# Weight pieces of the z/gates stage rounded and split in twos, one term's split moved, and the first eight o inputs rounded earlier

## The reference

```python
u = rms_norm(h, norm_g)
proj = u @ w_in                     # 1024 x 7168: q, f, i, g_hg, u_s, z_s, gate_hg, gate_s5
o = rms_norm(hgrn2_mix(q, f, i, lb), hg_norm_g)          # chunked recurrence, 8 heads
y_hg = (o * silu(g_hg)) @ w_o_hg
ys = gelu(s5_mix(u_s, ...))                              # 32 groups, 64 complex states each
ys = glu_a * sigmoid(glu_b) * silu(z_s)                  # glu_a, glu_b from ys @ w_glu + b_glu
y_s5 = ys @ w_o_s5
h = h + (sigmoid(gate_hg) * y_hg + sigmoid(gate_s5) * y_s5) @ w_out
h = h + (p @ w_ple) * sigmoid(rms_norm(h) @ w_ple_gate)
return rms_norm(h)
```

## Time and profile before

| what | value |
|---|---|
| median of 3 runs | 2148.1 us (2147.4 to 2154.41) |
| the profiled execution's own time | 2150.59 us |
| its span | 2149.0 us, mean granted TensorE clock 0.995 |
| PE busy | 2119.0 us (99%) |
| DVE busy | 1555.1 us (72%) |
| ACT busy | 1043.9 us (49%) |
| POOL busy | 292.8 us (14%) |

### The profile page before, as it was taken

The page is one execution under the profiler, slowest core; times in us unless marked ns, Lnnn a source line. Parts: engine busy times, 40 slices in busy tenths (PEclk is TensorE's granted clock), DMA queues, the critical chain, the costliest instruction groups (busy, mean ns, idle before and its releaser), DMA issues.

```text
span 2149.0 us, 29076 instructions
## 1 busy us (share of the span) xinstructions
PE 2119.0 (99%) x10178; PEld 1740.7 (81%) x10178; DVE 1555.1 (72%) x3140; ACT 1043.9 (49%) x1585; POOL 292.8 (14%) x518
## 2 busy tenths in 40 slices
PE   9999999999999999999998999999999999999997
PEld 6788888888888888888876788878888888888886
DVE  7775757777778778788888788566657567666756
ACT  6511245455455555575455455643544454354344
POOL 0011145000000000102322232211002001100100
PEclk9999999999999999999999999999999999999999
DMA  6453389311011011445568455675338435634632
GB/s 213 101 187 121 125 263 207 147 54 54 29 54 54 29 54 44 106 141 187 163 196 304 147 171 157 189 235 180 113 119 260 152 117 192 221 108 130 222 118 79
DMA packets 179598, 308.41 MB, mean 144 GB/s; under 512 B 40400, under 2 KB 85216, under 8 KB 179488
## 3 DMA queue, kind: packets, MB, share of 16 engines
q1 hardware_dynamic: 136816, 195.91, 28.6%
q0 software_dynamic: 38448, 102.69, 15.2%
q10 hardware_dynamic: 4224, 8.39, 1.1%
HBM read 232.33 MB, written 94.37 MB: 152 GB/s over the span
## 4 chain that ended last, share of the span: by engine, by line
PE 94%; DMA 2%; DVE 1%; ACT 1%; issue 1%; SPq 0%; DVEq 0%; ACTq 0%
PE c_bank L390 23%; PE c_bank L391 23%; PE c_bank L392 23%; PE c_bank L1499 6%; PE c_bank L1501 6%; PE c_bank L1500 6%; DMA u_hi<-terms_scratch 2%; PE c_bank L797 1%; PE c_bank L774 1%; PE c_bank L784 1%; PE c_bank L795 1%; PE c_bank L1536 1%; PE c_bank L1539 1%; PE c_bank L1519 1%; DMA x_xs<-x_in 0%
## 5 line engine op out<-in xcount | busy, mean ns | idle before, releaser
L390 PE MATMUL c_bank<-u_hi,c_w_both 128*128 128x512 f32 x576 | 231.9, 403 | 3.9 <-DVE u_hi L1181 1.7
L392 PE MATMUL c_bank<-u_hi,c_w_both 128*128 128x512 f32 x576 | 224.2, 389 | 0.0
L391 PE MATMUL c_bank<-u_lo,c_w_both 128*128 128x512 f32 x560 | 218.5, 390 | 0.0
L2308 ACT ACTIVATE c_w_both<-c_raw 128x1024 fp32r<-128x1024 f32 x91 | 96.6, 1061 | 166.5 <-PE c_bank L392 158.8
L1057 DVE STREAM_TRANSPOSE hg_ken<-hg_ke 32x128 f32<-32x128 f32 x512 | 154.6, 302 | 6.5
L390 PEld LDWEIGHTS c_bank<-u_hi,c_w_both 128*128 128x128 f32 x576 | 108.2, 188 | 34.4 <-issue 5.6
L391 PE MATMUL c_bank<-t_oa_lo,c_w_both 128*128 128x512 f32 (+1 forms) x344 | 132.1, 384 | 0.0
L392 PE MATMUL c_bank<-t_oa_hi,c_w_both 128*128 128x512 f32 (+1 forms) x344 | 132.1, 384 | 0.0
L390 PE MATMUL c_bank<-t_oa_hi,c_w_both 128*128 128x512 f32 (+1 forms) x344 | 132.1, 384 | 0.0
L392 PEld LDWEIGHTS c_bank<-u_hi,c_w_both 128*128 128x128 f32 x576 | 108.2, 188 | 23.0
L864 ACT ACTIVATE hg_S<-hg_G,hg_coef 128x128 f32<-128x128 f32 x120 | 47.5, 401 | 156.8 <-DVE hg_G L1082 110.9
(11 more groups left out here) (392 smaller groups left out, 5656.6 us busy)
## 6 DMA issues: line engine op xcount, KB each, us to landing
c_raw<-sums_scratch SPq DMA_DIRECT2D x80, 256.0 KB, 2.8
c_raw<-w_in_in SPq DMA_DIRECT2D x64, 256.0 KB, 3.8
gates_scratch<-s_stage POOLq DMA_DIRECT2D x64, 256.0 KB, 4.3
t_ein<-gates_scratch SPq DMA_DIRECT2D x64, 256.0 KB, 4.5
c_raw<-w_o_hg_in SPq DMA_DIRECT2D x32, 512.0 KB, 3.6
c_raw<-w_out_in SPq DMA_DIRECT2D x32, 512.0 KB, 3.3
c_raw<-w_ple_gate_in SPq DMA_DIRECT2D x32, 512.0 KB, 3.3
sums_scratch<-w_in_in POOLq DMA_DIRECT2D x60, 256.0 KB, 12.5
```

The costliest lines, as they stand in the source:

```text
L390: pe.matmul(out, w_hi, u_hi, start=first, stop=False)
L391: pe.matmul(out, w_hi, u_lo, start=False, stop=False)
L392: return pe.matmul(out, w_lo, u_hi, start=False, stop=last)
L2308: act.activation(w_hi[u % WS], raw[u % RS], ACT.Copy).then_inc(w_hi_done, 1)
```

## The change

It has three parts.

1. `round_piece` and `split_piece` do nothing for an even q. For an odd q they wait for both loads and handle the pieces q - 1 and q by one instruction over both slots (128x1024), which counts both semaphores up by 2. As `piece(u, i)` stands for 7u + i + 4, the instructions stand at i = 1, 3, 5 in even units and at i = 0, 2, 4, 6 in odd ones.
2. In unit 10 DVE's split of term 7 moves from behind `piece(u, 4)` to ahead of `piece(u, 2)` and `turn_forward`.
3. In the tail before its loop, o inputs 0 to 3 are rounded and split behind units 2 and 3 of `glu`, and 4 to 7 behind units 0 and 1 of `os5`; before, they stood behind units 0 to 3 of `os5`.

```diff
     def round_piece(self, act, q):
-        u, i = divmod(q, PRODS)
-        act.wait_ge(*self.piece_in[q % 4].at(16 * (q // 4 + 1)))
+
+        if q % 2 == 0:
+            return
+        for n in (q - 1, q):
+            act.wait_ge(*self.piece_in[n % 4].at(16 * (n // 4 + 1)))
         if q < 4:
             act.wait_ge(self.head_proj, 3 * (NT * HEADS - 1) + 1 + q // 2)
         else:
             act.wait_ge(*self.prod_done.at(q - 3))
-        act.activation(self.ring(q)[0], self.piece(q), ACT.Copy).then_inc(self.piece_hi.sem, 1)
+        hi, _, raw = self.both_pieces(q)
+        act.activation(hi, raw, ACT.Copy).then_inc(self.piece_hi.sem, 2)
 
     def split_piece(self, dve, q):
-        hi, lo = self.ring(q)
+        if q % 2 == 0:
+            return
+        hi, lo, raw = self.both_pieces(q)
         dve.wait_ge(*self.piece_hi.at(q + 1))
-        dve.tensor_tensor(lo, self.piece(q), hi.bitcast(F32), ALU.subtract).then_inc(self.piece_lo.sem, 1)
+        dve.tensor_tensor(lo, raw, hi.bitcast(F32), ALU.subtract).then_inc(self.piece_lo.sem, 2)
...
+                if u == 10:
+                    quads.split_term(dve, 7)
                 if u not in (0, 10):
                     piece(u, 2)
                 if use:
...
                 piece(u, 4)
-                if u == 10:
-                    quads.split_term(dve, 7)
                 gated(u, C11)
...
             if not body:
-                return [("o", 2 * i), ("o", 2 * i + 1)] if sec == "os5" else []
+                n = i - 2 if sec == "glu" else i + 2
+                return [("o", 2 * n), ("o", 2 * n + 1)] if 0 <= n < 4 else []
```

More of the change, by code:

```diff
@@ L250, with both_pieces @@
     SUM_DMAS, COPY_DMAS = NQ // 2 * 16, 2 * len(COPIED) * 16
+    def both_pieces(self, q):
+        r = q % 4 // 2
+        return self.w.hi[:, r], self.w.lo[:, r], self.w.raw[:, r]
     def round_piece(self, act, q):
-        u, i = divmod(q, PRODS)
-        act.wait_ge(*self.piece_in[q % 4].at(16 * (q // 4 + 1)))
+        if q % 2 == 0:
+            return
+        for n in (q - 1, q):
+            act.wait_ge(*self.piece_in[n % 4].at(16 * (n // 4 + 1)))
         if q < 4:
```

## The result

| | median | runs |
|---|---|---|
| before, measured with it on one chip | 2150.6 us | 2147.4 to 2154.41 (4) |
| changed kernel | 2172.36 us | 2170.96 to 2173.12 (4) |

A forecast was written before the change was run, and what follows sets the result against it. PE was taken as the bound, busy 2119.0 of 2149.0 us. The terms 3.8 + 4.2 + 1.7 + 0.5 + 0.2 - 1.8 gave +8.6 us, so 2156.7 against the median of 2148.1; range 2150.5 to 2163.

The forecast's parts named there:

- Even units, product 4: Six even z/gates units: the pair behind add_c11 starts product 4 late, 0.63 us each, 3.8 us in all.
- Odd units, product 5: Eight odd units, 3 to 17: the pair behind scans makes product 5 late, 0.52 us each, 4.2 us in all.
- Unit 0: Product 6's piece, formerly split ahead of term 3, now stands behind add_c11: 1.7 us later.
- Unit 2: Product 6's piece, formerly first of three, ends later as a pair: 0.5 us, lower bound 0.
- Unit 10: Product 6 waits for a pair behind turn_forward and the moved term 7 split: +0.2 us, bounds -0.8 and +1.5.
- The tail's o inputs: Tail: earlier splits remove PE's wait for o input 6, -1.8 us; bounds -1.8 and 0.
- ACT: ACT's round of a pair in z/gates units: begins early enough to leave over 3 us of cover, so no cost.
- Rival 4: Pairs of loads come late and ACT waits; eight units lose 1 us more each: 2165 us; chance 0.08.
- Rival 3: Clock falls at 14 new stalls, each costing one product at 1.2 GHz: +38 us, 2195 us; chance 0.02.
- Rival 2: Unit 10: earlier piece for product 6 halves the 7.28 us stall and keeps the clock up; 2140.0 us; chance 0.03.
- Rival 5: DVE's total decides: 70 x 0.07 = 5 us go, no stall comes; with the tail -6.7, 2141.4 us; chance 0.01.
- Rival 1: Even and odd units' small stalls too small to be seen, half of 8.0 goes: +4.6, 2152.7 us; chance 0.18.

The follow-up runs named there:

- e4: Changed kernel, loads in its order, but pairs stand earlier on DVE, in unit 10 ahead of the term's split; 2163.54 us, ratio 1.0069.
- e8: Kernel before, rounds and splits single, but SP's load of an even piece waits until both pieces in its two slots are split; 2161.2 us, ratio 1.0057.
- e9: Changed kernel with only unit 7's 2 MB copy load ahead of the load of piece 7u+7; 2166.54 us, ratio 1.0077.
- e1: Changed kernel, but in odd units SP issues U, trig and the copy ahead of the load of piece 7u+7; 2162.47 us, ratio 1.0064.
- e6: Kernel before with the change's third part alone, o inputs rounded and split earlier; 2148.2 us, ratio 0.9992.
- e2: Changed kernel, but in odd units SP loads piece 7u+8 ahead of U, trig and the copy, which stay late; 2163.9 us, ratio 1.0072.
- e5: Changed kernel with the load order of e1 and the pair places of e4 together; 2148.69 us, ratio 0.9994.
- e10: e5 with pieces 0 to 19 single again, pairs from piece 20 on; 2146.82 us, ratio 0.9986.
- e3: Kernel before with the change's second and third parts (term 7's split and o inputs earlier), no pairs; 2145.07 us, ratio 0.9983.

## Why the prediction was right or wrong

- **Even units, product 4**: right. 0.66 to 0.70 for a forecast of 0.63; the pair took the 1.22 us taken from the tail's rows.
- **Odd units, product 5**: place right, size too small. Product 5 began 0.47 to 0.54 late where the sum had 0.44, and 0.14 to 0.19 more was lost in the course of it, where the sum had 0.08: the first matmuls behind a stall follow each other in 0.34, then 0.24 and 0.23 us. In unit 3 product 4 was 0.16 late too. In units 15 and 17 the pair behind `matrices` stood 0.36 us later in the unit than in unit 13, which used up the 0.18 that I had to spare at product 3, and products 3 and 4 together were 0.35 late. 6.4 in place of 4.2. e4 shows the place to be the cause.
- **Unit 0**: right, 1.55 for 1.7. **Unit 2**: 1.4 for 0.5; DVE came to this unit's pair 0.9 later than I had it. It stood behind a result of ACT's (`par_lr`, L1611) until 4.96 us into the unit, 4.15 before.
- **Unit 10**: +0.2 forecast, -2.0 found. The stall at the unit's start gave the loads time, and product 5's wait of 2.74 was gone. Product 6 waited 8.8 us behind the pair, where I had 7.6. e8 and e9, which keep that stall, have the same 33.9 us for the unit. Where it was removed (e1), unit 10 cost 1.2 over before, inside my bounds, but no more than the unit varies by itself.
- **The tail's o inputs**: right, -1.8 on the wait list; its size in the time is not settled by e6.
- **The step that failed** is the one under **ACT**, "Over 3 us of cover remain". It reckoned when the round of a pair may begin by the product four before, and took the load as there, so it put at nothing what came to 13.45 of the 22 us: ACT stood 7.46 and 6.97 us before two rounds, and PE 5.11 and 4.61. I had counted instructions on DVE, ACT and PE, but not what the merged count does to SP: a split that frees two slots at once frees the first later, and in odd units a whole `matrices` later. SP waits for that in order, and U, trig, the copy and the next piece stand behind it. The rows of SP's queue in unit 7, which I had not read, show all of these behind that one wait.
- **Rival 4** named ACT waiting for late loads, with 0.08. Its end was right, its mechanism and size not: not eight units by 1 us but two by 6.7, where 2 MB of other loads had just been issued, and by SP's order (e2, e8, e9), not by two loads at once.
- **Rival 3**: stalls of 0.36 us left the clock up in all units, as forecast; the two of 5 us, which I had not foreseen, each drew the lower level behind them.
- **Rival 2**: e4 and e5 have what it asked for, the pair ahead of the term's split. Product 6's wait is 6.0 in e4 in place of 8.8, and 3.7 in e5: half of before's 7.28, as worked out. But unit 10 is only 2.1 us shorter in e5 than before, not 6.3, because the clock did not stay up. Before, product 5 followed a wait of 2.74 at full pace; in e5 it followed one of 2.49, the granted clock was 0.50 from 1176 to 1178, and the product took 4.8 us instead of 3.2. Product 6 ran at 0.50 again (1184 to 1188).
- **Rival 5** is refuted by e5 and e10: DVE has less to do and PE gets none of it. The Trainium skill, page "VectorE: DVE Perf Modes", section "The TRN2 errata — SBUF-src ops pay a fixed extra latency per instruction", says that one large tile pays a fixed cost once where small tiles pay it each. The traces agree as far as DVE goes (1555.1 to 1549.3 us busy, for 70 fewer); as a forecast of the time the rule would have had the wrong sign.
- **The sum and its range**: the ends of the range do not follow from the bounds beside them. Rival 1 with unit 10 at its low bound is 2151.7, and all the high bounds together are 2161.0, not 2150.5 and 2163; what was measured lies above either. Nor do all units of before repeat unit 13: in units 3 and 4 DVE splits its pieces 1.0 and 0.25 us later, which the sum left out.

Open is how much of unit 9's wait came from U and trig ahead of piece 71 and how much from the loads on ACT's queue: e2 took the first away, and the wait with it, but the two weren't varied apart. Nor does a run tell whether piece 57 was late because it stood behind the copy in the queue or because it shared the DMA engines with it (their share was 1.03, at 388 GB/s, from 1105 to 1110).

## What to carry to other kernels

Merging two instructions into one also merges the two releases that hang on it: follow the semaphore back to the queue that loads, and list what stands behind that wait in order. A ring of four slots that is freed in twos lets its next load go only when the later of two splits is done. A load queue should issue what needs no slot ahead of what waits for one, and an in-order engine that rounds weights should not stand in front of a load issued behind megabytes of others. Here 70 instructions saved on an engine that was 72% busy were worth nothing by themselves; what helped was to move the one split that was late.

## What the runs showed of the hardware

The clock does not answer a given pause in a given way. In unit 0 PE waits 2.24 us in the changed kernel and in e5 alike. Then, in the stretches after it (PE, PEld, DVE, ACT and POOL busy, clock, DMA share, GB/s), first the changed kernel, then e5:

```profile
950.00:952.50 2.50, 2.50 (x12) 2.04 (x12) 1.71 (x5) 1.61 (x6) 0.10 (x1) 1.00 0.70 118
952.50:955.00 2.50, 2.50 (x13) 2.07 (x12) 1.66 (x2) 1.68 (x3) 1.58 (x3) 1.00 0.71 275
```

```profile
950.00:952.50 2.50, 2.50 (x7) 1.99 (x6) 1.90 (x5) 1.61 (x6) 0.00 (x0) 0.50 0.78 161
952.50:955.00 2.50, 2.50 (x11) 1.98 (x10) 1.48 (x2) 1.12 (x3) 0.54 (x1) 0.86 0.70 259
```

The clock stays at 2.4 GHz in the one and falls to 1.2 GHz for some 3.5 us in the other, and this costs 1.6 us. e1 and e4 show the fall as well, e2 and e9 don't, with the same stall. Product 5 of unit 10 is alike: it ran at full pace behind waits of 2.74 (before) and 2.59 us (e6), and at the lower clock behind 2.09 (e1), 2.49 (e5), 2.54 (e10) and 2.63 (e3). The other surprise is the load's latency: 256 KB took 10.4 us from issue to landing behind the 2 MB copy on the same queue (changed kernel), and 4.5 without it (e9).
